# One of the seven products of the first FFN matrix computed by seven products over pairs of blocks, with its sums and low parts by VectorE and x1 kept in device memory

## What is computed

```python
x1 = _layer_norm(ALPHA * x + mix, ln1_g, ln1_b)
ff = jnp.square(jax.nn.relu(x1 @ w_ff1 + b_ff1)) @ w_ff2 + b_ff2
x2 = _layer_norm(ALPHA * x1 + ff, ln2_g, ln2_b)
```

## Time and profile before

| | |
|---|---|
| median of 3 runs | 1053.3 us (1053.25 to 1054.08) |
| time of the profiled execution | 1053.31 us |
| its span, first to last instruction | 1051.5 us |
| TensorE busy (matmul) | 1041.0 us, 99% of the span, 7797 matmuls |
| VectorE busy | 719.3 us, 68% |
| ScalarE busy | 486.6 us, 46% |
| GpSimd busy | 87.5 us, 8% |
| mean granted TensorE clock | 0.998 |

### The profile page before, as it was taken

One profiled execution on the slowest core, in us unless ns is written; L12 is line 12 of the kernel. 1 busy time (PEld: TensorE's weight loads), 2 busy tenths in 40 slices (PEclk: granted clock), 3 DMA queues, 4 the chain that ended last, 5 costly groups with the idle time before them and its releaser, 6 DMA issues. The chain is left out here.

```text
span 1051.5 us, 18890 instructions
## 1 busy us (share of the span) xinstructions
PE 1041.0 (99%) x7797; PEld 1028.1 (98%) x7797; DVE 719.3 (68%) x956; ACT 486.6 (46%) x685; POOL 87.5 (8%) x120
## 2 busy tenths in 40 slices
PE   9999999999999999999999999999999999999997
PEld 9999999999899999999999999999999999999985
DVE  6795775536786595855655655658766677887977
ACT  6554434445532576645454554556443323334223
POOL 3112221020211000000000000000000000000027
PEclk9999999999999999999999999999999999999999
DMA  8546996164225211254345345387524415335304
GB/s 284 144 173 156 246 199 130 61 176 114 91 80 159 83 41 55 78 171 152 120 155 165 110 151 168 122 284 254 206 82 151 172 62 182 121 92 171 122 5 157
DMA packets 95154, 148.34 MB, mean 141 GB/s; under 512 B 6164, under 2 KB 51956, under 8 KB 94568
## 3 DMA queue, kind: packets, MB, share of 16 engines
q1 hardware_dynamic: 88290, 127.72, 38.1%
q0 software_dynamic: 6528, 19.19, 7.9%
q10 hardware_dynamic: 270, 0.49, 0.2%
HBM read 104.19 MB, written 49.06 MB: 146 GB/s over the span
## 5 line engine op out<-in xcount | busy, mean ns | idle before, releaser
L2340 PE MATMUL bank<-x_hi,w_hi 128*128 128x344 f32 (+1 forms) x696 | 227.5, 327 | 0.2 <-DVE x_lo L1616 0.2
L2340 PE MATMUL bank<-x_hi,d_lo 128*128 128x258 f32 x968 | 222.4, 282 | 0.0
L2340 PE MATMUL bank<-x_lo,w_hi 128*128 128x344 f32 (+1 forms) x696 | 222.0, 319 | 0.0
L2340 PE MATMUL bank<-x_hi,w_lo 128*128 128x344 f32 x528 | 168.7, 319 | 0.0
L2340 PEld LDWEIGHTS bank<-x_hi,d_lo 128*128 128x128 f32 x968 | 165.7, 189 | 0.0
L2340 PEld LDWEIGHTS bank<-x_hi,w_hi 128*128 128x128 f32 (+1 forms) x696 | 130.4, 187 | 0.9 <-DVE x_lo L1616 0.5
L2340 PEld LDWEIGHTS bank<-x_lo,w_hi 128*128 128x128 f32 (+1 forms) x696 | 130.2, 187 | 0.4
L2340 PE MATMUL bank<-x_lo,s_hi 128*128 128x258 f32 x448 | 126.5, 282 | 0.0
L2340 PE MATMUL bank<-x_hi,s_hi 128*128 128x258 f32 x448 | 126.4, 282 | 0.0
L2340 PEld LDWEIGHTS bank<-x_hi,w_lo 128*128 128x128 f32 x528 | 99.2, 188 | 0.0
L2340 PE MATMUL bank<-t_hi,s_hi 128*128 128x258 f32 x336 | 95.2, 283 | 0.0
(11 more groups left out here) (400 smaller groups left out, 2432.3 us busy)
## 6 DMA issues: line engine op xcount, KB each, us to landing
h_ops<-h_unit SPq DMA_DIRECT2D x56, 258.0 KB, 2.5
x_lo_raw<-h_ops SPq DMA_DIRECT2D x14, 1032.0 KB, 5.3
s_raw<-in_w_ff SPq DMA_DIRECT2D x14, 1024.0 KB, 6.8
x_lo_raw<-h_ops SPq DMA_DIRECT2D x14, 774.0 KB, 4.5
d_raw<-in_w_ff SPq DMA_DIRECT2D x9, 1024.0 KB, 7.8
w_raw<-in_w_in SPq DMA_DIRECT2D x16, 512.0 KB, 7.3
h_ops<-t_out SPq DMA_DIRECT2D x28, 258.0 KB, 5.2
d_raw<-in_w_ff SPq DMA_DIRECT2D x8, 768.0 KB, 6.3
```

The costliest lines, as they stand in the source:

```text
L2340: return nc.tensor.matmul(out, lhsT, rhs, start=start, stop=stop, skip_group_check=True)
```

## The change

In the six pairs of units 1 to 6 the two products with X21 (one in each unit of a pair) are replaced. The two units' weight blocks side by side (512 x 256) and X21 (512 x 516) are cut once more into 2 x 2 blocks of 256 x 128 and 256 x 258, and seven small products (`inner`, 2 chunks x 3 parts = 6 matmuls of 258 columns each) take the place of the 48 matmuls. All seven stand in the first unit of the pair (`up_first`), in two half banks `IN_A` and `IN_B` of the former `PC`; the second unit (`up_second`) has six products left, in the order X11, X12, XT2, X22, XT3, XT4. The result for the second unit is gathered in SBUF (`UPB`).

- VectorE makes the four sums of small weight blocks (`iw_sums`) and their low parts (`iw_los`) for the next pair during `up_second`; `s_lo_12` shrinks to half, since that weight block's quarter is split with the small blocks. The add into h11 is split into adds of 258 columns between the small products.
- ScalarE makes the high parts of the small blocks (`iw_hi_raw`, `iw_hi_sums`) and copies two half banks to `UPB`; its `s_hi_12` shrinks to half too.
- GpSimd loads the small weight blocks once more (`load_iw`, two transfers of 256 KB each pair), and makes the sums of blocks of x1 and their low parts once, during units (0,0) and (0,1).
- `Y` gives its room to the new tiles: GpSimd stores x1 (4 MB) in device memory before the units and reads it back at the end of the last pair, before `d_add` needs it.
- In `up_second`, VectorE and ScalarE work in another order than in `up_unit`, and SyncE stores h11 before h22.

The diff, cut to its core:

```diff
@@ SyncE, store_unit
+                if j and r:
+                    sp.wait_ge(sq_even, n(1, 1))
+                    store(j, r, B11, HT[:, 0:1, 0:HALF])
                 sp.wait_ge(sq_22, n(1, 1))
                 store(j, r, B22, HT[:, 1:2, HALF:NT])
...
@@ GpSimd
+            pool.wait_ge(xv_ready, KC * NBLK)
+            for i in range(4):
+                pool.dma_start(y_d[:, 2 * i:2 * i + 2, :], Y[:, 2 * i:2 * i + 2, :]).then_inc(y_out, 16)
+            pool.wait_ge(y_out, DMA0 + 64)
+            pool.wait_ge(t_sum, 5)
+            load_iw(1)
...
+            G.tensor_tensor(T1S[:, :, :], b12, b11, ALU.subtract).then_inc(iw_sum, 1)
+            pool.wait_ge(iw_sum, IS0 + 1)
+            G.tensor_tensor(TPR[:, 0, :, :], b22, T1S[:, :, :], ALU.subtract).then_inc(iw_sum, 1)
+            G.tensor_tensor(TPR[:, 1, :, :], b22, b12, ALU.subtract).then_inc(iw_sum, 1)
...
+            with pool.Fori(1, NSU // 2 - 1) as j:
+                pool.wait_ge(in_done, at_pair(j)(IN0, N_IN, 7))
+                load_iw(j, 1)
+            pool.wait_ge(in_done, at_pair(NSU // 2 - 1)(IN0, N_IN, 7))
+            for i in range(3):
+                pool.dma_start(Y[:, 2 * i:2 * i + 2, :], y_d[:, 2 * i:2 * i + 2, :]).then_inc(y_in, 16)
...
@@ ScalarE, up_second
+                act.wait_ge(up_done, n(7, 3))
+                act.wait_ge(up_added, n(3, 1))
+                A(halves(TMP[:, 0, :]), pair_sum(PD), ACT.Copy).then_inc(up_copied, 1)
...
+                if not last:
+                    s_hi_12(m, 0, 1)
+                    iw_hi_raw(j, 1)
...
+                act.wait_ge(up_added, n(3, 2))
+                hidden_even(n, r)
+                if not last:
+                    s_hi_34(m, 0)
+                    iw_hi_sums(j, 1)
...
+                act.wait_ge(up_added, n(3, 3))
+                hidden_22(n, r)
@@ VectorE, up_first
+                s_lo_5(n, 0)
+                dve.wait_ge(in_done, q(IN0, N_IN, 1))
...
+                V.tensor_tensor(h11a, TMP[:, 0, 0:HB], IN_A, ALU.add).then_inc(in_added, 1)
...
+                V.tensor_tensor(h11a, h11a, IN_B, ALU.add).then_inc(in_added, 1)
+                s_lo_6(n, 0)
+                s_sums(m, 1)
+                dve.wait_ge(in_done, q(IN0, N_IN, 3))
+                V.tensor_tensor(h11b, TMP[:, 0, HB:HALF], IN_A, ALU.add).then_inc(up_added, 1)
+                s_lo_7(n, 0)
+                s_lo_12(m, 1, 1)
@@ VectorE, up_second
+                s_lo_5(n, 1)
...
+                s_lo_7(n, 1)
+                if not last:
+                    s_lo_12(m, 0, 1)
+                    iw_sums(j, 1)
...
+                V.tensor_tensor(halves(HT[:, 0, HALF:NT]), halves(TMP[:, 1, :]), pair_sum(PD), ALU.add).then_inc(up_added, 1)
...
+                V.tensor_tensor(HT[:, 1, HALF:HALF + HB], TMP[:, 0, 0:HB], PA[1][:, 0, 0:HB], ALU.add).then_inc(in_added, 1)
+                dve.wait_ge(up_done, n(7, 6))
+                V.tensor_tensor(HT[:, 1, HALF + HB:NT], TMP[:, 0, HB:HALF], PA[1][:, 1, 0:HB], ALU.add).then_inc(up_added, 1)
+                if not last:
+                    s_lo_34(m, 0)
+                    iw_los(j, 1)
+                else:
+                    w_lo_part(0)
+                    h_lo_part(0)
...
@@ TensorE, up_first
+                product(PA[0], hi(0), raw_lo(0), *X11, True, False, n_done=2)
+                pe.wait_ge(up_added, n(3, -2))
+                pe.wait_ge(iw_lo, q(IL0 + 2, 2, 1))
+                inner(IN_A, W11, Q11, True, False)
+                inner(IN_B, W12, Q21, True, True)
...
+                product(PA[0], hi(2), sum_lo(0), *XT2, False, False)
...
+                inner(IN_A, WS2, QT2, False, False)
...
+                inner(IN_B, WS1, QT1, True, False)
...
+                product(PD, hi(3), sum_lo(1), *X12, True, False)
+                pe.wait_ge(up_added, n(3, 1))
+                inner(IN_A, WS3, QT3, False, False)
...
+                product(PA[0], hi(0), raw_lo(2), *XT3, False, False)
...
+                inner(IN_B, WS4, Q22, False, True)
...
+                product(PD, hi(1), sum_lo(2), *X22, False, True)
...
+                inner(IN_A, W22, QT4, False, True)
...
+                product(PA[0], hi(2), raw_lo(3), *XT4, False, True)
@@ TensorE, up_second
...
+                product(PA[1], hi(0), raw_lo(2), *XT3, False, False, first_half=in_done)
+                pe.wait_ge(s_lo, n(5, 5))
+                pe.wait_ge(in_added, q(AD0, N_AD, 5))
+                product(PA[1], hi(2), raw_lo(3), *XT4, False, True, second_half=(up_added, n(3, 3)))
```

More of the change, by code:

```diff
@@ L1197, in s_hi_34, with up_unit @@
                 A(SH[r][:, 2:4, :], SS[r][:, 0:2, :], ACT.Copy).then_inc(s_hi, 1)
-            def up_unit(j, r, first=False, last=False):
+            def up_unit(j, r, first=False):
                 n, m = at_unit(j, r), at_unit(j, r + 1)
@@ L1294, in _ @@
             with act.Fori(1, NSU // 2 - 1) as j:
[L1295 to L1298, removed]
+                up_first(j)
+                up_second(j)
+            up_first(NSU // 2 - 1)
+            up_second(NSU // 2 - 1, last=True)
             h_hi_part(1)
@@ L2020, in up_unit @@
                 s_lo_6(n, r)
-                if not last:
-                    s_sums(m, 1 - r)
+                s_sums(m, 1 - r)
                 s_lo_7(n, r)
-                if not last:
-                    s_lo_12(m, 1 - r)
+                s_lo_12(m, 1 - r, 2 - r)
+                if r:
+                    iw_sums(1)
                 dve.wait_ge(up_done, n(7, 5))
@@ L2029, in up_unit @@
                 V.tensor_tensor(halves(HT[:, 1, HALF:NT]), halves(TMP[:, 0, :]), pair_sum(PA[r]), ALU.add).then_inc(up_added, 1)
[L2030 to L2034, removed]
+                s_lo_34(m, 1 - r)
                 dve.wait_ge(up_done, n(7, 6))
@@ L2259, in _ @@
             with dve.Fori(1, NSU // 2 - 1) as j:
[L2260 to L2263, removed]
+                up_first(j)
+                up_second(j)
+            up_first(NSU // 2 - 1)
+            up_second(NSU // 2 - 1, last=True)
             w_lo_part(1)
             h_lo_part(1)
+            dve.wait_ge(y_in, DMA0 + 64)
             d_add(1, 0)
@@ L2655, in classical, with product @@
                               lambda k: XH[:, k, blk(b)], lambda k: XL[:, k, blk(b)], range(KC)).then_inc(gemm_done, 1)
-            def product(out, w_hi, w_lo, x_hi_, x_lo_, start, stop):
+            def product(out, w_hi, w_lo, x_hi_, x_lo_, start, stop, n_done=1, first_half=None, second_half=None):
                 for i in range(2):
+                    if i and first_half is not None:
+                        last.then_inc(first_half, 1)
+                    if i and second_half is not None:
+                        pe.wait_ge(*second_half)
                     o, ns = out[:, i, 0:HB], slice(HB * i, HB * (i + 1))
@@ new lines, in _, with inner @@
+            QT2, QT3, QT4 = ((TPH[:, x, :, :], TPL[:, x, :, :]) for x in range(3))
+            W11, W12, WS3, W22 = ((IWH[:, x, :], IWRL[:, x, :]) for x in range(4))
+            WS1, WS2, WS4 = ((IWH[:, 4 + x, :], IWSL[:, x, :]) for x in range(3))
+            def inner(out, w, x, start, stop):
+                for k in range(2):
+                    cs = slice(P * k, P * (k + 1))
+                    mm(out, w[0][:, cs], x[0][:, k, :], start and k == 0, False)
+                    mm(out, w[0][:, cs], x[1][:, k, :], False, False)
+                    last = mm(out, w[1][:, cs], x[0][:, k, :], False, stop and k == 1)
+                last.then_inc(in_done, 1)
@@ L2801, in _ @@
             with pe.Fori(1, NSU // 2) as j:
-                for r in range(2):
-                    up_unit(j, r)
+                up_first(j)
+                up_second(j)
             for t in range(NOP * len(GROUPS)):
```

261 lines of the change are left out of this document (240 added, 21 removed).

## The result

The changed kernel takes **1109.5 us** (median of 6 runs, 1109.0 to 1113.9) against 1053.3 of the kernel before in the same session: ratio 1.054, 95% interval 1.0529 to 1.0551. Slower, as forecast, but by twice as much: 1081 was given, with a range from 1063 to 1096.

What follows compares the result with a forecast made beforehand. The prediction took the kernel as the sum of TensorE's matmuls (busy 99%). Its terms, -4.3 + 20.0 + 5.0 + 1.7 + 1.5 + 3.5 = +27.4 on 1053.3, gave 1080.7 us, range 1063 to 1096.

Steps and rivals of the forecast that it cites:

- The add behind the sums: In `up_first`, the add into h11's second half follows four weight sums on VectorE; WS3 stalls 1.4 us before any slip.
- the slipped hidden sums: In `up_second`, the third hidden sum ends 5.2 us after the unit, not 2.6; next weights come 2.6 later.
- The -4.3 for the matmuls: Six pairs lose 6 matmuls each, 36 at 0.120 us: -4.3 us.
- rival A: TensorE's clock falls behind the 4.0 us stalls, the next product runs at 1.2 GHz: 14.4 us more, 1095; chance 0.15.
- the ring: In each pair, a cycle of load, sums, adds, ScalarE, hidden sums, load again; pair period 44.6 us instead of 40.3.
- Each pair has two loads in its cycle: Both weight loads of a pair were taken at 6.9 us from issue to first use; bounds 5.5 and 8.0.
- at nothing: Terms priced at zero: x1's 4 MB store, GpSimd's small loads (0.5 MB a pair), ScalarE's extra high parts not counted elsewhere.
- GpSimd's sums: Sums of x1 beside VectorE in unit (0,0): free if both run freely, 3.3 us if they block; middle taken, +1.5 us.
- the entry: Before pair 1, TensorE waits after X11 for the small blocks' first low part, behind VectorE's fourth hidden sum: +1.7 us.
- The exit: Last unit: wait before the second matrix, at least 2.5 us, plus reading x1 back; between 2.5 and 8, taken +3.5 us.
- The stall per pair: 4.0 us before WS3 in pairs 2 to 6 (+20.0), 1.0 us before XT4 in pairs 1 to 5 (+5.0).
- Rivals B and C: B: hidden sums don't slip, 1065, chance 0.08. C: not slower, weights in SBUF by 8.5 us, 1053.2, chance 0.03.

Runs made afterwards that it cites:

- e6: The kernel before, with 36 matmuls left out of the product with X21 in the last 12 units: 1048.7 us against 1053.5.
- e9: The changed kernel, with SyncE issuing the next unit's weight load ahead of the three stores of hidden sums instead of behind them: 1079.7 us.
- e1: The changed kernel, with VectorE's add of h11's second half put ahead of the four weight sums in the first unit of a pair: 1089.6 us.
- e3: The changed kernel, with GpSimd's load of the next small blocks held back until the next unit's weights have landed: 1109.5 us.
- e2: The changed kernel, with unused filler matmuls before two waits: 16 before WS3 in the first unit of a pair, 15 before XT4 in the second: 1113.6 us.
- e5: The changed kernel, with x1's small sums and low parts made by VectorE instead of GpSimd: 1103.1 us.
- e4: The changed kernel, with x1 read back only after TensorE has ended the last FFN unit: 1107.7 us.
- e7: As e1, with VectorE's small-block sums and low parts also ahead of the weight sums, and ScalarE's high parts of them earlier: 1077.3 us.

## Why the prediction was wrong

**The sign and the mechanism held.** The add behind the sums, the slipped hidden sums, 14.7 from landing to next load, 3.05 from landing to WS3: all within 0.3 us. So is the load 5.6 us into the unit in pairs 2 to 4; in pairs 5 and 6 it goes out at 4.6 and 4.2. The -4.3 for the matmuls was right for a stream that TensorE bounds (e6), and e9 and e1 show that the two causes named, the load's place and the add's, are the causes.

**What failed is the size of four terms; none of them alone.** The sum gave 27.4 where 55.9 came.

- *The clock, rival A, was an alternative with a chance of 0.15 and belonged in the sum.* It fell behind most of the stalls, and A's sign, values under 9 in PEclk, is on the page. Its price of 14.4 rested on 24 slow matmuls behind each of five stalls; there were 16 to 21 behind four. Of the 17.0 us of extra busy time 6.6 are inside the ring; the rest lies elsewhere, 3.0 of it behind XT4. So A's event came, at less than half of its price inside the ring, and the forecast held none of it.
- *"Each pair has two loads in its cycle", both at 6.9.* The small blocks' 0.5 MB were put under "at nothing". They make the second unit's load 8.3 (e3: 7.2 without them): with 6.7 for the other, +4.7 us from unit (2,0) to the last unit. With the clock's 6.6 that is 11.3 of the 13.8 missed there. Most of the other 2.5 is in two pieces of the ring: WS3 to the load 13.4 where the clock holds (e2) against 13.1, and landing to load 14.9 against 14.7, in each of four turns.
- *GpSimd's sums and the entry, 1.5 and 1.7.* The stalls ahead of pair 1 were 4.8 us (1.3, 0.5, 0.3 and 2.65): more than the 3.3 of the upper end, since not only the sums but the later low part blocked a hidden sum, and the load behind it. The Trainium skill (SBUF — State Buffer, "SBUF: two separate sides") has GpSimd and such a VectorE operation exclude each other for a whole instruction. The trace agrees: the hidden sum started at 451.11 ends 0.6 us after GpSimd's low part, and e5 takes these stalls away. The low part for pair 1 cost 0.9, not 1.7. XT4's first wait of 2.6 instead of 1.0 and 1.1 us of slow matmuls from 469.5 on bring the account to 5.2 of the 7.1; the other 1.9 was not taken apart.
- *The exit, 3.5, "near the lower end".* The waits came to 9.1 (7.0 and 2.1). The lower end was right (2.1 in e4 against 2.5); the reading cost 7.0, above the 5.8 at which half of it was reckoned. I had priced bytes; what the rows show are two stores and a weight load that landed late beside it, on which VectorE and ScalarE wait in turn.

The stall per pair, 4.0 and 1.0, came out as 3.1 and 2.6, which looks like compensation but is not. The 2.6 is mostly the longer load. Before WS3 the waits are 3.5 to 3.9 in pairs 2 to 4, as forecast, and 2.3 and 2.0 in pairs 5 and 6, where slow matmuls behind XT4 bring TensorE 1.5 us later to the next WS3. With the clock up and the fillers counted as waits (e2) the two are 4.3 and 2.6. **The range** was built from bounds that were each taken alone; 1096 was the value of rival A with all other terms in the middle, though a fallen clock and longer loads do not exclude each other. Rivals B and C didn't occur: the load came late in every first unit, and in none were the weights there by 8.5 us.

## What to carry to other kernels

When a stall is forecast, find the ring that it belongs to and write down its length: engine time outside the ring is free, inside it is paid in full, and every transfer that shares the ring's load is in it too. An event that follows from the forecast itself (long stalls, hence a lower clock) goes into the sum, priced by the part of it inside the ring. And before splitting a product further, look at where the loads are issued: the order of instructions on SyncE or VectorE was worth 20 to 32 us here (e1, e9, e7), the arithmetic saved 4.

## What the runs showed of the hardware

- Two loads of 256 KB on GpSimd's queue made a 1 MB load on SyncE's queue 8.3 us instead of 7.2, and the issue of it 0.5 to 0.8 us instead of 0.46.
- A 1 MB load issued ahead of five stores of 258 KB took 9.3 us where it took 8.3 behind three of them, with the small loads beside it both times; without them 6.6 and 6.7, so the stores alone do not explain it.
- VectorE and GpSimd, both with operands in SBUF, stretched each other: 3.92 for a hidden sum of 0.70, and on GpSimd 3.15 for 516 columns where the first such operation took 1.12.
- Filling waits with matmuls held TensorE's granted clock at 1.00 from 570 to 630 us and gave 1113.6 us instead of 1109.5: 1.5 us came back in most turns between WS3 and the next load, and longer loads took it away again.
